# The rounded and the low part of every transposed left side, interleaved element by element

## The reference

```
# first block, twice
h = rms_norm(x, g_pre) * (1.0 + scale) + shift
proj = h @ w_in                  # 2048 x 5648
... (sliding window attention, spatial gating, gated linear attention)
out = y @ w_out                  # 2048 x 2048
x = x + gate * rms_norm(out, g_post)
# second block, twice
proj = h @ w_in                  # 2048 x 3648
q = rms_norm(c_q) @ w_uq ; kv = rms_norm(c_kv) @ w_ukv
... (three attention mixers)
x = x + mixed @ w_o              # 2048 x 2048
x = x + square(relu(h @ w_up)) @ w_down   # 2048 x 8192 and back
```

## Time and profile before

| | |
|---|---|
| median of 3 runs | 3006.74 us (3000.99, 3006.74, 3007.43) |
| span of the profiled execution, first to last instruction | 3004.9 us |
| TensorE clock granted, mean | 0.989 of full |
| PE / PEld / DVE / ACT busy | 96% / 81% / 63% / 49% of the span |
| HBM | 202 GB/s over the span |

### The profile page before, as it was taken

The page is one execution under the profiler, slowest core; times in us unless marked ns, Lnnn a source line. Parts: engine busy times, 40 slices in busy tenths (PEclk is TensorE's granted clock), DMA queues, the critical chain, the costliest instruction groups (busy, mean ns, idle before and its releaser), DMA issues.

```text
span 3004.9 us, 35050 instructions
## 1 busy us (share of the span) xinstructions
PE 2881.6 (96%) x13692; PEld 2427.2 (81%) x13692; DVE 1878.9 (63%) x2387; ACT 1479.2 (49%) x2038; POOL 48.6 (2%) x60
## 2 busy tenths in 40 slices
PE   4998897999999999999999999999999999999998
PEld 4886776788888888788888888888887888888887
DVE  7897998668855557655545554545566555445554
ACT  4436544565546655644334444455546443344443
POOL 0000000000000000000000000000000000000000
PEclk9999998999999999999999999999999999999999
DMA  9995697857655544566566666565455666666664
GB/s 369 333 345 180 217 313 283 278 183 247 233 170 164 171 144 149 169 185 186 191 194 191 185 185 195 179 177 163 140 160 169 187 186 191 193 189 188 199 194 140
DMA packets 297717, 609.66 MB, mean 203 GB/s; under 512 B 19360, under 2 KB 81072, under 8 KB 296912
## 3 DMA queue, kind: packets, MB, share of 16 engines
q1 hardware_dynamic: 295584, 600.42, 63.3%
q0 software_dynamic: 1824, 6.61, 0.7%
q10 hardware_dynamic: 144, 0.39, 0.0%
HBM read 605.24 MB, written 2.10 MB: 202 GB/s over the span
## 4 chain that ended last, share of the span: by engine, by line
PE 83%; DVE 7%; ACT 4%; DMA 3%; issue 2%; SPq 0%; POOL 0%; POOLq 0%; ACTq 0%; DVEq 0%
PE ps L1871 26%; PE ps L1878 26%; PE ps L1874 26%; DMA raw<-in_w_in 2%; PE ps L1830 2%; DVE w_lo L1177 2%; PE ps L1996 1%; DVE raw L1285 1%; PE ps L1980 1%; ACT w_hi L839 1%; PE ps L1888 1%; ACT probs L1041 1%; DMA raw<-in_w_modT 1%; DVE x L1266 0%; DVE smax L1446 0%
## 5 line engine op out<-in xcount | busy, mean ns | idle before, releaser
L1177 DVE TENSOR_TENSOR w_lo<-raw,w_hi 128x1024 fp32r<-128x1024 f32 (+4 forms) x988 | 1158.2, 1177 | 974.1 <-ACT w_hi L839 970.8
L839 ACT ACTIVATE w_hi<-raw 128x1024 fp32r<-128x1024 f32 (+4 forms) x988 | 1003.6, 1019 | 1237.1 <-PE ps L1878 1057.0
L1871 PE MATMUL ps<-w_hi,hT_hi 128*128 128x512 f32 (+3 forms) x2848 | 766.5, 391 | 37.2 <-ACT hT_hi L920 19.2
L1874 PE MATMUL ps<-w_lo,hT_hi 128*128 128x512 f32 (+3 forms) x2848 | 741.6, 382 | 0.6 <-DVE w_lo L1177 0.6
L1878 PE MATMUL ps<-w_hi,hT_lo 128*128 128x512 f32 (+3 forms) x2848 | 739.0, 381 | 0.0
L1871 PEld LDWEIGHTS ps<-w_hi,hT_hi 128*128 128x128 f32 x2848 | 521.0, 190 | 128.5 <-issue 25.6
L1874 PEld LDWEIGHTS ps<-w_lo,hT_hi 128*128 128x128 f32 x2848 | 536.4, 190 | 91.7 <-DVE w_lo L1177 0.8
L1878 PEld LDWEIGHTS ps<-w_hi,hT_lo 128*128 128x128 f32 x2848 | 534.9, 189 | 90.4
L1871 PE MATMUL ps<-w_hi,uT_hi 128*128 128x512 f32 x1024 | 275.9, 391 | 0.0
L1874 PE MATMUL ps<-w_lo,uT_hi 128*128 128x512 f32 x1024 | 274.5, 389 | 0.0
L1878 PE MATMUL ps<-w_hi,uT_lo 128*128 128x512 f32 x1024 | 274.5, 389 | 0.0
(11 more groups left out here) (246 smaller groups left out, 1475.8 us busy)
## 6 DMA issues: line engine op xcount, KB each, us to landing
raw<-in_w_up SPq DMA_DIRECT2D x256, 512.0 KB, 3.7
raw<-in_w_down SPq DMA_DIRECT2D x256, 512.0 KB, 3.7
raw<-in_w_modT SPq DMA_DIRECT2D x192, 512.0 KB, 5.6
raw<-in_w_in SPq DMA_DIRECT2D x128, 456.0 KB, 3.5
raw<-in_w_in SPq DMA_DIRECT2D x88, 512.0 KB, 4.9
raw<-in_w_out SPq DMA_DIRECT2D x64, 512.0 KB, 4.7
raw<-in_w_o SPq DMA_DIRECT2D x64, 512.0 KB, 3.7
raw<-in_w_in SPq DMA_DIRECT2D x64, 450.0 KB, 6.4
```

The source lines that it names most:

```text
L839: act.activation(w_hi[:, L % SPLIT_SLOTS, 0:c, 0:w], raw[:, G % RAW_SLOTS, 0:c, 0:w], ACT.Copy).then_inc(S.hi_ready, 1)
L1177: dve.tensor_tensor(w_lo[:, r, 0:c, 0:w], raw[:, r, 0:c, 0:w], w_hi[:, s, 0:c, 0:w].bitcast(F32), ALU.subtract).then_inc(S.group_read, 1)
L1871: pe.matmul(o, rows(hi, c, t), wh[c], start=start and c == 0, stop=False)
L1874: pe.matmul(o, rows(hi, c, t), wl[c], start=False, stop=False)
```

## The change

Each pair of buffers becomes one buffer with a last dimension of two, and the hi and lo names become views on it with a step of two elements (8 bytes). Sizes and addresses of all other buffers stay.

```
-        hT_hi = sb("hT_hi", [P, KC, 2 * P], F32R)
-        hT_lo = sb("hT_lo", [P, KC, 2 * P], F32R)
+        hT_pair = sb("hT_pair", [P, KC, 2 * P, 2], F32R)
+        hT_hi, hT_lo = (hT_pair[:, :, :, part] for part in range(2))
...
-        cT_hi = A2q("cT_hi", [P, 4, 2 * P], F32R)
-        cT_lo = A2q("cT_lo", [P, 4, 2 * P], F32R)
+        cT_pair = A2q("cT_pair", [P, 4, 2 * P, 2], F32R)
+        cT_hi, cT_lo = (cT_pair[:, :, :, part] for part in range(2))
...
-        uT_hi = A2m("uT_hi", [P, UPC // P, 2 * P], F32R)
-        uT_lo = A2m("uT_lo", [P, UPC // P, 2 * P], F32R)
+        uT_pair = A2m("uT_pair", [P, UPC // P, 2 * P, 2], F32R)
+        uT_hi, uT_lo = (uT_pair[:, :, :, part] for part in range(2))
```

## The result

The changed kernel takes 3052.41 us (median of four runs, 3051.02 to 3053.99) against 3004.01 us before (four runs, 3000.99 to 3007.43). The ratio is 1.016, with a 95% interval of 1.0148 to 1.0173: 48 us slower. The forecast of no change was wrong. The time lies inside the stated range, but between the two cases that the range was drawn around, no change and the half-rate load, and at neither of them: that it lies inside is luck, not a confirmation of the working.

The account below looks back on a forecast made before the run. PE bounds the kernel: number of matmuls times the distance between starts. Instructions, left-side loads and writers summed as 0 + 0 + 0, leaving 3007 us; range 2999 to 3086 us.

Parts of the forecast that it names:

- no change: Whole kernel: the step of two costs nothing, span stays at 3004.9 us, median 3007 us; chance 0.69.
- the half-rate load: Rival, left-side loads: each takes 222 ns, felt at 456, 450 and 344 columns, +71 us, 3078 us; chance 0.15.
- What bounds the kernel: Three lines of the product on PE: time is the number of matmuls, 11,772, times the distance between starts.
- How much a load may cost: Left-side loads: 111 ns each at most, so 2.04 times slower before a matmul of 512 columns (227 ns) feels it.
- The load of the left side: 11,772 loads reading 8 bytes apart instead of 4: factor 1, price 0; at factor 1.8, 25 us.
- The lower bound: Left-side loads: price at least nothing, since a stepped load can't be quicker and a quicker one, already hidden, gains nothing.
- The signs of being wrong: Profile after: load records off 188 to 190 ns, or bursts of four 512-column matmuls not 0.91 us apart.
- The comparison of the two read paths: PE's reads: a stepped load walks 2.3 words per ns, as the moving side always does, so it costs nothing extra.
- The page on cachelines: SBUF lines of 16 bytes need two hits for full bandwidth; a float32 step of two gives two, so 0.
- The writers: ACT's line 920 and DVE's lines 1370, 1379, 1381: factor 1, times stay at 632 and 687 to 692 ns, price 0.
- The rival of slow writers: ACT's writes at factor 1.8 and the low parts behind them lengthen six PE waits: +6 us, 3013 us; chance 0.05.
- far slower one: Rival, left-side loads: 2.5 times slower, 278 ns, every product load-bound, +686 us, about 3691 us; chance 0.05.

Follow-up runs that it names:

- the bursts: Kernel before with bursts of 16 equal matmuls behind its last product, left side's step and width varied: 512 columns take 226.7 ns at step 1, 232.6 at step 2.

## Why the prediction was wrong

**What bounds the kernel**: right. The span is the number of matmuls times their distance. No wait moved by more than 2.5 us.

**How much a load may cost**: right in the load's own time, wrong in what follows from it, that it could get 2.04 times as slow before 512 columns felt it; 1.05 times was enough (next paragraph). A load in a row occupies its path for 112 ns (111 had been read). At a step of four it takes 233 ns, the rival's half-rate load. The sum made in the same way as the rival's, with the distances from the bursts (that for 450 columns set between its neighbours), came out at 197 us against 193 measured (3196.93 - 3003.6).

**The load of the left side**: this is the step that failed, "Price at factor 1: 0". The factor itself was nearly right, 118 / 112 = 1.05. The error is in taking a load that fits under its matmul as one that costs nothing. The distance of 227 ns in the earlier trace rows is 13 ns more than 512 columns at 2.4 GHz take (213), and I didn't ask what these 13 ns were. Five are there whatever the two sides' steps, and 8 come with a moving side that walks through memory while a left side is loaded. With a step of two in the left side these 8 are 14. A term of +6.4 ns x 8892, less 4.3 ns x 1536, was missing. No row of before gave its size, but the rows with 456 columns gave a hint: 209 - 190 = 19 ns of excess, not 13. An excess that isn't the same for all widths is neither a fixed cost nor the clock. The lower bound had the same fault: "a quicker load would gain nothing anyway" and "no step of the change saves time on PE", but 456 columns did get 4 ns closer. The signs of being wrong that the prediction named did come: load records of 193 to 196 ns instead of 188 to 190, and bursts 0.93 us apart instead of 0.91.

**The comparison of the two read paths**: its conclusion was wrong. "The load needs nothing that the moving side doesn't get" looked at what each side gets alone. Both are read at once. The moving side itself gets only half its rate at a step of two (450 ns), so one word in two is not what it "does all the time". A lone word costs 450 / 512 = 0.88 ns on the moving side and 118 / 128 = 0.92 ns in a load. The load at step one already took 0.87 ns per word, and so it loses almost nothing.

**The page on cachelines** ("SBUF — State Buffer" of the Trainium skill, cachelines): its rule of two hits on a line agrees for the load's own rate (112, 118, then 233 ns at a step of four). It doesn't agree for the moving side, which halves its rate at a step of two although each line is hit twice. The note says nothing on two reads at once, and that is what decided here.

**The writers**: DVE as predicted, 693 ns. ACT's factor is 1.06, not 1, and hidden as the text said. The rival of slow writers is refuted at a step of two: the six waits grew by 2.5 us in all. Even at a step of four, with ACT at the factor 1.8 that the rival assumed, they are 21.9 us, so its +6 us was too much. The row behind that factor was not about lone words alone either: in the trace before, the predicated copy takes 1.30 us at level 2 as well (334.02 us), in runs of two, and 0.71 only from level 3 on.

**The rivals**: no half-rate load and no far slower one at a step of two; at a step of four the half-rate load is what happens. I had given 0.71 to no change. That the range held the time anyway comes from having stretched it up to the half-rate load, which did not happen. The missing case was a price of a few ns at each of 11,772 places, which the list of rivals had only as an aside ("a few ns of hand-over at 512 columns").

## What to carry to other kernels

Before a hidden load is priced at zero, compare the distance between matmuls with width / 2.4: what is above it can be a price of the loads already, and a layout can change it in either direction. Where some ten thousand equal instructions set the time, 1 ns in their distance is 10 us, so put a range of a few ns on it instead of a zero. A stationary fp32r operand may be read with a step of two at about the rate of a row, but from a step of four on its load takes about twice as long (217 to 267 ns against 112). A moving operand should be read in a row.

## What was not expected of the hardware

- The distance between matmuls of fp32r depends on the addresses: 226.7 to 233.2 ns at 512 columns as the left side moves by 0 to 256 words, with all else the same.
- It depends on the width unevenly. With a step of two, 488 columns and 480 columns take the same 220 ns.
- A burst of equal matmuls can take up to eleven of them to settle into a repeating pattern, and many of the settled distances are multiples of 6.67 ns.
- A moving side at a step of two takes 450 to 454 ns for 512 columns, and at a step of four 460 to 464. A left side that repeats one word doesn't take the excess away; a moving side that repeats one word does.
- At a step of four, writes slow down by 1.8 on ACT (632 to 1142 ns) and 1.6 on DVE (692 to 1124 ns), while at a step of two they cost 6% and nothing.
- What in the memory makes the two reads meet, by banks or otherwise, stays open: the bursts show where the time goes, not the circuit.
